# A diffusion step's first stages: finer pieces, column tiles in S5, and its weights made between the short convolutions

## The chip, the cores and the metric

One core of one Trainium2 chip. The metric is the device time of one execution of the whole step, in microseconds (us), median of three runs.

## The reference, cut to what matters

One inference step of a two-layer trunk. Layer 0 (even) mixes 640 tokens (128 of context, 512 latent) with two mixers side by side, a Hyena long convolution and an S5 scan; layer 1 is an mLSTM; each layer has an expert mixer. The change touches what comes before the first expert mixer.

```python
def hyena_filters(n_tok, w1, b1, w2, b2, w3, freq, decay):
    ...
    h = jnp.sin(fr * (z @ _f(w1) + _f(b1)))
    h = jnp.sin(fr * (h @ _f(w2) + _f(b2)))
    h = (h @ _f(w3)) * jnp.exp(-t[:, None] * jnp.abs(_f(decay)))
    h = h.reshape(n_tok, HY_ORDER, 2, HY_WIDTH)
    fwd, bwd = h[:, :, 0], h[:, :, 1]
    kern = jnp.concatenate([fwd, jnp.zeros_like(fwd[:1]), bwd[1:][::-1]], axis=0)
    kern = kern * lax.rsqrt(jnp.sum(kern * kern, axis=0, keepdims=True) + EPS)
    return jnp.fft.rfft(kern, axis=0)

def s5_mix(u, h0_re, h0_im, a_re, a_im, b_re, b_im, c_re, c_im, log_step, d_skip, glu_w, glu_b):
    ...
    lam_bar = jnp.exp(lam * jnp.exp(_f(log_step))[..., None])
    b_bar = ((lam_bar - 1.0) / lam)[..., None] * lax.complex(_f(b_re), _f(b_im))
    ...
    y_f, hf = s5_scan(u, lam_bar[0], b_bar[0], c_mat[0], h0[:, 0])
    y_b, hb = s5_scan(u[:, ::-1], lam_bar[1], b_bar[1], c_mat[1], h0[:, 1])
    y = (y_f + y_b[:, ::-1]).reshape(bsz, n_tok, S5_WIDTH) + _f(d_skip) * u_flat
    y = jax.nn.gelu(y)
    y = y * jax.nn.sigmoid(y @ _f(glu_w) + _f(glu_b))
```

`lam_bar` depends on weights alone: 32 groups of 16 channels with 64 complex states in each of two directions. Beside this, `silu(cond) @ ada_w` gives the scales and shifts of all norms.

## The kernel before, in words

The program is a chain of stages; a stage is a block in which each engine has its own list of instructions, written out by hand, with semaphores between the lists. Nothing reorders a list. The residual stays in the tile `X` (128 x 5 x 1024, f32), the tokens in five tiles of 128.

`start` (L915 to L1232) makes the Hyena filters' spectra, the first quarter of the conditioning and the first norm. PE: two sine layers (L1004), per token tile four raw tap products of 512 columns (L1035) into four banks, with one block of the conditioning (L1015) behind each of the first four; then the context's spectrum (L1058), eight blocks of the DFT (L1072) with the column sums of squares (L1048) between them, and a product that spreads the norms over the partitions (L1080). DVE: the sines' reduction (L1149, L1238 to L1244), the taps (L1158 to L1164), squares (L1171), spectra (L1182), the first norm (L1189, L1192), and last ten multiplications of the spectra `KC`, `KS` by their norms (L1231). ACT: sines, envelopes, copies, square sums of `X` (L1127). POOL adds the position embedding to `X` in one operation (L999).

`even_inputs` (L1262 to L1425) transposes the normed rows into `HT` (L1334), multiplies by 16 blocks of 128 columns of the input weights (L1314, each block 16 matmuls of 320 tokens), convolves the first 12 blocks with three taps on DVE (`short_conv`, L1252 and L1256), turns them on PE (L1325) and places them. The last four blocks are S5's channels; ACT drains each in 16 pieces of 32 x 160 (L1389) that sort the tokens by their place in a chunk of four. After the convolutions DVE makes S5's parameters (`s5_parameters`). `hyena_convolve` follows.

`s5` (L1697 to L2167) works in four quads of groups. For a quad m DVE makes the input weights (`inputs`, L2048 to L2054) and the readout weights (`readouts`, L2071 to L2085), PE transposes the input weights (`turn`), maps chunks into states (`into_states`, L1971), DVE turns the states by angles (`turn_in`, L2095 to L2114), scans them (L2124) and turns back (`scans`, L2136 to L2159, which ends with `prev_set`), PE makes the matrix inside a chunk (`inside`, L1982) and the outputs (`outputs`, L1999, L2002), ACT applies Gelu in 16 pieces (L1892). POOL makes the angles and decays of each quad. Between these steps PE takes the remaining 16 blocks ("rows") of the conditioning product (`ada_row`, L1935), whose weights SP streams from DRAM through two buffers.

DVE's order in `s5` is: inputs(0), diagonal, inputs(1), readouts(0), turn_in(0), scans(0), then for each m turn_in(m), readouts(m), inputs(m + 1), scans(m). PE's is: turn(m), row, into_states(m), row, outputs(m - 1), row, inside(m), row.

`s5_gate` and `project_and_norm` follow; the latter adds the projected mix to `X`.

## Time and profile before

| | |
|---|---|
| median of three runs | 4515.22 us (4513.23 to 4517.06) |
| profiled execution | 4515.3 us, span 4513.5 us |
| mean granted clock of TensorE | 0.968 |
| busy share of the span: PE, DVE, POOL, ACT | 93%, 65%, 36%, 17% |
| `start` | 0 to 150.5 us |
| `even_inputs` | 150.5 to 308.3 us |
| `hyena_convolve` | 308.3 to 412.7 us |
| `s5` | 412.7 to 645.4 us |
| `s5_gate` | 645.4 to 667 us |

### The profile page before, as it was taken

The numbers are of one execution on the slowest core, as the hardware profiler recorded it, in microseconds if no ns is written. First come the engines' busy times: TensorE is split into PE (matmuls) and PEld (weight loads), VectorE is DVE, ScalarE is ACT, GpSimd is POOL, SyncE is SP. The second block draws the span as 40 slices with busy tenths as digits, with TensorE's granted clock in tenths as the row PEclk, the third lists the DMA queues.
The fourth block names the chain that finished last, engine by engine and source line by source line (L and its number), as shares of the span: only waits on it lengthen the run. The fifth ranks groups of instructions, "written<-read, shape, count | busy, mean of one in ns | idle before, by whom it ended". The sixth has DMA issues, their size and how long they took to land. (4 is left out here: it accounts for less than half of the span.)

```text
span 4513.5 us, 44328 instructions
## 1 busy us (share of the span) xinstructions
PE 4206.5 (93%) x15630; PEld 2476.9 (55%) x15630; DVE 2955.5 (65%) x5889; ACT 751.1 (17%) x1583; POOL 1619.6 (36%) x1472
## 2 busy tenths in 40 slices
PE   7785669999999999999989997999999999999998
PEld 3552445768554555545536875576855455554553
DVE  5447953999876766557634227499987676664763
ACT  2121441037000000000002222102810000000000
POOL 1003300028566655545400000001956564554640
PEclk9897889999999999999999999999999999999999
DMA  4111641137999999979921204112789999997993
GB/s 166 52 58 39 228 182 58 56 107 223 364 357 365 410 360 365 353 293 410 350 86 56 70 28 91 41 57 85 223 338 363 366 410 360 363 361 287 406 359 119
DMA packets 354408, 1045.42 MB, mean 232 GB/s; under 512 B 31657, under 2 KB 132361, under 8 KB 343002
## 3 DMA queue, kind: packets, MB, share of 16 engines
q0 software_dynamic: 148096, 545.34, 31.7%
q1 hardware_dynamic: 107036, 447.12, 26.8%
q10 hardware_dynamic: 99072, 50.33, 4.0%
q8 instruction: 116, 1.90, 0.2%
q14 instruction: 88, 0.72, 0.0%
HBM read 988.54 MB, written 54.14 MB: 231 GB/s over the span
## 5 line engine op out<-in xcount | busy, mean ns | idle before, releaser
L592 PE MATMUL banks<-blocks,picked_T 128*128 128x512 f32 x3072 | 1359.1, 594 | 16.0 <-DVE picked_T L772 16.0
L555 PE MATMUL banks<-h_dense_T,blocks 128*128 128x384 f32 x4096 | 1357.6, 486 | 0.0
L555 PEld LDWEIGHTS banks<-h_dense_T,blocks 128*128 128x128 f32 x4096 | 776.9, 190 | 581.9 <-issue 98.5
L592 PEld LDWEIGHTS banks<-blocks,picked_T 128*128 128x128 f32 x3072 | 585.9, 191 | 711.6 <-issue 657.5
L383 POOL DMA_INDIRECT expert_rows<-in_pk_u_dram,expert x512 | 667.3, 1303 | 478.6 <-DVE own_dots L787 253.7
L383 POOL DMA_INDIRECT expert_rows<-in_pk_v_dram,expert x512 | 601.1, 1174 | 514.5 <-DVE acc L806 262.4
L806 DVE SCALAR_TENSOR_TENSOR acc<-expert_rows,expert_weight,acc 128x1024 f32<-128x1024 f32 x504 | 622.8, 1282 | 67.4 <-DMA expert_rows<-in_pk_v_dram,expert 66.8
L787 DVE CUSTOM_DVE_ANT_0 expert_rows<-expert_rows,h_rows 128x1024 f32<-128x1024 f32 x512 | 601.5, 1221 | 59.1 <-DMA expert_rows<-in_pk_u_dram,expert 57.6
L772 DVE TENSOR_TENSOR picked_T<-dense_act,shared 128x384 f32<-128x384 f32 x246 | 209.9, 854 | 569.6 <-PE banks L592 560.1
L408 ACT ACTIVATE dense_act<-banks 128x384 f32<-128x384 f32 x246 | 120.6, 490 | 2229.8 <-PE banks L555 2229.6
L374 POOL TENSOR_SCALAR expert_rows<-iota,picked_T 128x128 f32<-128x128 f32 x384 | 251.2, 672 | 472.7 <-ACT picked_T L414 415.9
L761 DVE TENSOR_SCALAR expert_rows<-iota,picked_T 128x128 f32<-128x128 f32 x768 | 222.0, 364 | 9.7 <-PE banks L581 9.4
L535 PE MATMUL banks<-h_dense_T,blocks 128*128 128x384 f32 x512 | 210.9, 494 | 2.9 <-PEq L107 2.9
L581 PE MATMUL banks<-expert_rows 128*128 128x128 f32 x1536 | 181.8, 277 | 20.0 <-ACT expert_rows L428 11.8
L581 PEld LDWEIGHTS banks<-expert_rows 128*128 128x128 f32 x1536 | 175.8, 192 | 28.8 <-ACT expert_rows L428 16.0
L537 PE MATMUL banks<-shared,blocks 128*128 128x256 f32 x512 | 154.2, 383 | 0.0
L2696 POOL MEMSET VX<- 128x40 f32 x1 | 0.2, 169 | 420.3 <-POOLq L107 420.3
L361 POOL IOTA iota<- 128x16 f32 x2 | 0.3, 146 | 409.8 <-POOLq L107 409.8
L1314 PE MATMUL banks<-HT,MIXT 128*128 128x320 f32 x512 | 140.1, 433 | 1.0 <-ACT HT L1371 1.0
L2464 PE MATMUL banks<-w_block,shared 128*128 128x256 f32 x640 | 138.3, 379 | 0.0
L2443 PE MATMUL banks<-shared,w_block 128*128 128x320 f32 x512 | 138.0, 432 | 0.0
L537 PEld LDWEIGHTS banks<-shared,blocks 128*128 128x128 f32 x512 | 98.6, 193 | 69.6 <-issue 3.3
(495 smaller groups left out, 3788.7 us busy)
## 6 DMA issues: line engine op xcount, KB each, us to landing
blocks<-in_pk_u_turned_dram SPq DMA_DIRECT2D x256, 512.0 KB, 6.6
blocks<-in_pk_v_dram SPq DMA_DIRECT2D x256, 512.0 KB, 6.7
gates_dram<-shared ACTq DMA_DIRECT2D x48, 1024.0 KB, 5.1
shared<-gates_dram SPq DMA_DIRECT2D x32, 1536.0 KB, 11.4
ada_block<-in_ada_rest_dram SPq DMA_DIRECT2D x32, 1280.0 KB, 7.5
blocks<-in_pk_w_q_dram SPq DMA_DIRECT2D x32, 512.0 KB, 3.4
MIXT<-in_ev_w_in_dram SPq DMA_DIRECT2D x16, 512.0 KB
expert_rows<-in_pk_u_dram,expert POOLq DMA_INDIRECT x512, 8.4
```

What stands on the lines that cost most here:

```text
L374: pool.tensor_scalar(hot(first_hot, n), iota128[:], cols[:, z, 0, t:t + 1], None, ALU.is_equal).then_inc(hot_first, 1)
L383: pool.indirect_dma_start(out=rows[:, r % RING, :], out_offset=None, in_=table, in_offset=bass.IndirectOffsetOnAxis(ap=idx[:, x, n % SLOTS ...
L535: pe.matmul(ps[:, at_:at_ + DENSE], lhs, HT[:, k, :], start=(k == 0), stop=(k == KD - 1))
L537: mm = pe.matmul(ps[:, at_ + HALF:at_ + HALF + NR * P], lhs, HTR[:, k, :], start=(k == 0), stop=(k == KD - 1))
L555: mm = pe.matmul(dense_dots(c), u[:, k * P:(k + 1) * P], HT[:, k, :], start=(k == 0), stop=(k == KD - 1))
L581: pe.matmul(ps[:, at_:at_ + P], hot(second_hot, n), hot(first_hot, n), start=True, stop=True).then_inc(spread, 1)
L592: mm = pe.matmul(ps[:, at_:at_ + HALF], wt[:, c % WEIGHED, z * P:(z + 1) * P], v[:, half_ * HALF:(half_ + 1) * HALF], start=(c == 0), stop ...
L761: dve.tensor_scalar(hot(second_hot, n), iota128[:], cols[:, z, 1, t:t + 1], cols[:, z, 2, t:t + 1], ALU.is_equal, ALU.mult).then_inc(hot_s ...
L772: dve.tensor_tensor(wt[:, c % WEIGHED, :], activation_of(c), gate_of[g % 2][:, :, c % KEYS_A_GROUP], ALU.mult).then_inc(weighed, 1)
L787: dve.tensor_tensor_reduce(rows[:, r % RING, :], rows[:, r % RING, :], H[:, x, :], 1.0, 0.0, ALU.mult, ALU.add, dots[:, x, n:n + 1]).then_ ...
L806: ins = dve.scalar_tensor_tensor(out=a, in0=rows[:, r % RING, :], scalar=by, in1=a, op0=ALU.mult, op1=ALU.add)
L1314: mm = pe.matmul(ps[:, at + c * HALF:at + c * HALF + EVEN], lhs, HT[:, k, c * EVEN:(c + 1) * EVEN], start=(k == 0), stop=(k == KD - 1))
```

## The change

1. `start`. The first sine layer waits for three loads on two queues (SP and ACT) instead of six on one; the layers run in halves of 320 columns. Raw taps come in ten units of 2 x 512 columns that rotate through three pairs of banks; envelopes likewise. The position embedding is added by DVE in four pieces between the taps. The last two conditioning blocks follow all raw taps. Squares move from DVE to ACT; the column sums use four column tiles of 32; DVE's steps for the norm are reordered. The ten multiplications of `KC` and `KS` move to the beginning of `even_inputs` on DVE.
2. `even_inputs`. SP first stores `X` to DRAM. DVE's loop over the blocks is written out, and between the twelve convolutions DVE makes S5's parameters, the input weights of all quads (kept in a tile of their own) and the readout weights (kept in `X`'s place). The last four blocks are made by `chunk_products`: 128 matmuls of 32 x 160 in four column tiles, whose moving operand reads every fourth token; ACT drains each block in one operation.
3. `hyena_convolve` reuses a tile in place of one of its own.
4. `s5`. DVE clears `BL`, makes the first quad's angles and the diagonal, and no inputs or readouts; ACT copies these into place (`place_inputs`, `place_readouts`, `begin`). POOL makes the angles of the other quads. The first quad's `into_states` is ahead of its two conditioning rows. Conditioning rows, `inside` and `outputs` use column tiles of 32; their drains are one or two ACT operations instead of 4 or 16, and a row is stored by two transfers.
5. SP loads `X` back from DRAM when the last readouts are placed; DVE waits for that at the beginning of `project_and_norm`.

The core of the diff:

```diff
@@ start
+            act.dma_start(w1[:], T["hy_w1"]).then_inc(first_in, 16)
+            act.dma_start(col[:], T["hy_cols"]).then_inc(first_in, 16)
-            pool.wait_ge(x_in, 32)
-            pool.tensor_tensor(X[:, 1:NT, :], X[:, 1:NT, :], pos, ALU.add).then_inc(x_ready, 1)
+            def raw(u):
+                t, o = divmod(u, 2)
+                if u >= 3:
+                    pe.wait_ge(taps_done, u - 2)
+                for d in range(2):
+                    j, at = 2 * o + d, raw_at(u) + d * HALF
+                    mm = pe.matmul(ps[:, at:at + HALF], h[:, t * P:(t + 1) * P],
+                                   w3[:, j * HYW:(j + 1) * HYW], start=True, stop=True)
+                mm.then_inc(taps_raw, 1)
...
+                    mm = pe.matmul(ps[32 * q:32 * q + 32, SUMS:SUMS + P],
+                                   one_at[:, 31 - row:63 - row], sq[:, n * P:(n + 1) * P],
+                                   start=(t == 0 and n < 4), stop=(t == NT - 1 and n >= 2 * KD - 4))
...
+            for t in range(NT):
+                taps(t)
+                if t == 1:
+                    dve.wait_ge(x_in, 32)
+                if t:
+                    dve.tensor_tensor(X[:, t, :], X[:, t, :], pos[:, t - 1, :], ALU.add
+                                      ).then_inc(x_ready, 1)
@@ even_inputs
+            sp.dma_start(x_dram, X[:]).then_inc(x_kept, 16)
+            def chunk_products(i, b):
+
+                pe.wait_ge(w_in[b], 16 * i + 16)
+                pe.wait_ge(x_out, 2 * i + (b - 1))
+                for n in range(4):
+                    at = (2 * b + n // 2) * HALF + n % 2 * CHUNKS
+                    for k in range(KD):
+                        lhs = w[:, b, k * P + 32 * n:k * P + 32 * n + 32]
+                        for j in range(T4):
+                            mm = pe.matmul(ps[32 * j:32 * j + 32, at:at + CHUNKS], lhs,
+                                           HT[:, k, j::T4], start=(k == 0), stop=(k == KD - 1))
+                mm.then_inc(used, 1)
...
-                for k in range(4):
-                    for j in range(T4):
-                        ins = act.activation(
-                            UP[32 * j:32 * j + 32, m, k, :].rearrange("p (h c) -> p h c", h=2),
-                            src[32 * k:32 * k + 32, :, j::T4], ACT.Copy)
-                ins.then_inc(x_out, 1)
+                act.activation(UP[:, m].rearrange("p (h k) c -> p h (k c)", h=2), src, ACT.Copy
+                               ).then_inc(x_out, 1)
...
+            turns()
+            for c in range(hyena):
+                b = c % 2
+                dve.wait_ge(x_out, c + 1)
+                dve.wait_ge(turned, c + 1)
+                short_conv(dve, line, y[:, b, :], x[:, b, :], lambda k: taps[:, c, k:k + 1])
+                dve.sem_inc(conv_done, 1)
+                dve.sem_inc(x_used, 1)
+                if c == 0:
+                    decays()
+                elif c == 1:
+                    powers()
+                elif c == 2:
+                    weights()
+                elif c < 7:
+                    inputs(c - 3)
+                elif c < 11:
+                    if c == 7:
+                        dve.wait_ge(x_kept, 16)
+                    readouts(c - 7)
@@ s5
+            sp.wait_ge(c_set, 8 * QUADS)
+            sp.dma_start(X[:], x_dram).then_inc(x_in, 16)
+                for j in range(T4):
+                    at = y_at(j)
+                    for i in range(4):
+                        pe.matmul(ps[32 * i:32 * i + 32, at:at + CHUNKS], M[:, i, 32 * j:32 * j + 32],
+                                  UP[:, m, i, :], start=True, stop=False)
+                    for d in range(2):
+                        for part in range(2):
+                            for i in range(4):
+                                mm = pe.matmul(ps[32 * i:32 * i + 32, at:at + CHUNKS],
+                                               CL[:, part, 4 * d + i, 4 - 4 * d + j, :],
+                                               PREV[:, part, 4 * d + i, :], start=False,
+                                               stop=(d == 1 and part == 1))
+                    mm.then_inc(y_raw, 1)
...
+                to = G[:, m, :].rearrange("p (c j) -> p j c", j=T4)
+                for n in range(2):
+                    src = ps[:, y_at(2 * n):y_at(2 * n) + 2 * CHUNKS]
+                    act.activation(to[:, 2 * n:2 * n + 2, :], src.rearrange("p (j c) -> p j c", j=2),
+                                   ACT.Gelu_apprx_tanh).then_inc(y_out, 1)
-            inputs(0)
-            dve.wait_ge(diag_set, 1)
-            inputs(1)
             for m in range(QUADS):
-                if m == 0:
-                    readouts(0)
                 turn_in(m)
-                if m:
-                    readouts(m)
-                    if m + 1 < QUADS:
-                        inputs(m + 1)
                 scans(m)
@@ project_and_norm
+            dve.wait_ge(x_in, 16)
```

PE's list at the end of `even_inputs`, before; `HT` holds the transposed rows, `MIXT` the weights' buffers, `conv_block` a convolved block:

```order
L1314 MATMUL banks<-HT_0,MIXT_0 128x320 x16
L1325 MATMUL banks<-ident_0,conv_block_0 128x128 x5
L1314 MATMUL banks<-HT_0,MIXT_0 128x320 x16
L1325 MATMUL banks<-ident_0,conv_block_0 128x128 x5
L1314 MATMUL banks<-HT_0,MIXT_0 128x320 x32
```

and with the change:

```order
L1392 MATMUL banks<-HT_0,MIXT_0 32x160 x128
L1402 MATMUL banks<-ident_0,conv_block_0 128x128 x5
L1392 MATMUL banks<-HT_0,MIXT_0 32x160 x128
L1402 MATMUL banks<-ident_0,conv_block_0 128x128 x5
L1392 MATMUL banks<-HT_0,MIXT_0 32x160 x256
```

A block of 16 matmuls has become 128, in the same place among the turns.

DVE's list at the beginning of `s5`, before, from the inputs of quad 1 to the first turn (`norm_rows` holds readouts and tables, `s5_w` are work tiles):

```order
L2048 TENSOR_TENSOR s5_w_1_0<-s5_B_0,s5_powers_in_0 128x512
L2049 TENSOR_TENSOR s5_w_3_0<-s5_B_0,s5_powers_in_0 128x512
L2054 TENSOR_TENSOR s5_Bl_0<-s5_w_1_0,s5_w_3_0 64x32x16 x2
L2071 TENSOR_TENSOR s5_w_1_0<-s5_C_0,s5_powers_out_0 128x640
L2072 TENSOR_TENSOR s5_w_3_0<-s5_C_0,s5_powers_out_0 128x640
L2085 TENSOR_TENSOR norm_rows_0<-s5_w_1_0,s5_w_3_0 64x4x5x16 x4
L2078 TENSOR_TENSOR s5_w_1_0<-s5_C_0,s5_powers_out_0 128x640
L2079 TENSOR_TENSOR s5_w_3_0<-s5_negC_0,s5_powers_out_0 128x640
L2085 TENSOR_TENSOR norm_rows_0<-s5_w_3_0,s5_w_1_0 64x4x5x16 x4
L2095 TENSOR_TENSOR s5_w_0_0<-MIXT_0,norm_rows_0 128x8x32
```

and with the change, from the second operation of the stage to the first of the turn (the angles are L2217 to L2224):

```order
L2217 TENSOR_TENSOR norm_rows_1<-s5_steps_0,s5_turns_0 128x1024
L2218 TENSOR_SCALAR norm_rows_1<-norm_rows_1 128x1024
L2219 TENSOR_SCALAR norm_rows_1<-norm_rows_1 128x1024
L2220 TENSOR_TENSOR norm_rows_1<-s5_steps_0,s5_turns_0 128x1024
L2221 TENSOR_TENSOR norm_rows_1<-s5_steps_0,s5_turns_0 128x1024
L2222 TENSOR_TENSOR norm_rows_1<-norm_rows_1 128x1024
L2223 TENSOR_TENSOR norm_rows_1<-norm_rows_1 128x1024
L2224 TENSOR_SCALAR norm_rows_1<-norm_rows_1 128x1024
L2227 MEMSET states_before_0 128x2x4
L2228 MEMSET states_before_0 128x2x4
L2229 TENSOR_TENSOR s5_diag_0<-ident_0,s5_d_0 32x512
L2239 TENSOR_TENSOR s5_w_0_0<-MIXT_0,norm_rows_1 128x8x32
```

The inputs and readouts have left this list; the angles have come to it from POOL's.

DVE's list in `even_inputs` with the change, from one convolution past a quad's readouts to the next (before, there was nothing between two convolutions but a copy of the taps):

```order
L1306 TENSOR_SCALAR conv_block_0<-conv_source_0,conv_taps_0 128x640
L1310 SCALAR_TENSOR_TENSOR conv_block_0<-conv_source_0,conv_taps_0,conv_block_0 128x127
L1310 SCALAR_TENSOR_TENSOR conv_block_0<-conv_source_0,conv_taps_0,conv_block_0 128x511
L1310 SCALAR_TENSOR_TENSOR conv_block_0<-conv_source_0,conv_taps_0,conv_block_0 128x127
L1310 SCALAR_TENSOR_TENSOR conv_block_0<-conv_source_0,conv_taps_0,conv_block_0 128x511
L1586 TENSOR_TENSOR MIXT_0<-s5_C_0,s5_powers_out_0 128x640
L1587 TENSOR_TENSOR MIXT_0<-s5_C_0,s5_powers_out_0 128x640
L1588 TENSOR_TENSOR X_0<-MIXT_0 128x640
L1589 TENSOR_TENSOR MIXT_0<-s5_C_0,s5_powers_out_0 128x640
L1590 TENSOR_TENSOR MIXT_0<-s5_C_0,s5_powers_out_0 128x640
L1591 SCALAR_TENSOR_TENSOR X_0<-MIXT_0 128x640
L1306 TENSOR_SCALAR conv_block_0<-conv_source_0,conv_taps_0 128x640
```

Six operations of readouts, two of which write `X`, have come in between.

## Rows read from the trace of the kernel before

**Rows 1.** The page's chain that ended last: share of the span by line.

```profile
PE banks L555 15%; PE banks L592 15%; ACT expert_rows L423 1%; PE banks L581 0%; DVE top_index L646 0%; DVE top_index L650 0%; PE banks L535 0%; DVE rest L647 0%; DMA gates_dram<-shared 0%; ACT shared L441 0%; DVE top_value L644 0%; DVE top_value L649 0%; PE banks L537 0%; ACT expert_rows L428 0%; DVE best_at L646 0%
```

**Rows 2.** Windows by stage: length, busy PE, PEld, DVE, ACT, POOL; clock, DMA, GB/s.

```profile
0.00:150.50 150.50, 99.29 (x576) 49.29 (x576) 92.95 (x88) 34.84 (x52) 13.61 (x13) 0.87 0.33 124
150.50:308.30 157.80, 151.07 (x612) 109.41 (x612) 55.09 (x182) 42.79 (x114) 0.00 (x0) 0.99 0.25 79
...
412.70:645.40 232.70, 130.64 (x1666) 92.49 (x1666) 196.22 (x242) 108.09 (x276) 83.69 (x43) 0.76 0.50 187
```

**Rows 3.** Timeline of `start`, the sine layers: PE, DVE, ACT.

```profile
8.34 1.96 PE L1004 MATMUL banks<-features,hy_w 33*64 33x512 f32 x2 [8.34 <-DMA hy_times<-in_hy_times_dram]
...
10.86 0.94 DVE L1149 TENSOR_SCALAR sine_arg<-banks,hy_cols 64x640 f32<-64x640 f32 x1 [2.29 <-PE banks L1005]
...
22.71 0.74 ACT L1093 ACTIVATE sine<-sine_arg 64x640 f32<-64x640 f32 x1 [6.77 <-DVEq L1152]
```

**Rows 4.** Timeline of `start`, the taps: DVE and POOL.

```profile
30.79 1.22 DVE L1158 TENSOR_TENSOR taps<-banks,envelope 128x1024 f32<-128x1024 f32 x1 [8.17 <-PE banks L1035]
...
41.18 9.47 POOL L999 TENSOR_TENSOR X<-X,MIXT 128x4096 f32<-128x4096 f32 x1
...
41.87 9.87 DVE L1164 TENSOR_TENSOR taps<-taps,bwd_taps 128x1024 f32<-128x1024 f32 x1
...
72.69 1.22 DVE L1164 TENSOR_TENSOR taps<-taps,bwd_taps 128x1024 f32<-128x1024 f32 x1
```

**Rows 5.** Timeline of `start`, sums, DFT, spread and the last multiplications.

```profile
84.14 3.67 PE L1048 MATMUL banks<-envelope,one_column 128*16 128x128 f32 x32
...
87.74 3.70 PE L1072 MATMUL banks<-taps,cos_fwd 128*128 128x512 f32 x8
...
127.45 3.69 PE L1080 MATMUL banks<-envelope,ones 16*128 16x512 f32 x8
...
137.93 1.22 DVE L1231 TENSOR_TENSOR KC<-KC,banks 128x1024 f32<-128x1024 f32 x1
```

**Rows 6.** Timeline of `even_inputs`: PE and SP at its start, DVE, ACT's last drain.

```profile
150.59 5.92 PE L1334 MATMUL banks<-ident,MIXT 128*128 128x128 f32 x40 [19.44 <-PEq L107]
157.51 14.80 PE L1314 MATMUL banks<-HT,MIXT 128*128 128x320 f32 x54 [1.00 <-ACT HT L1371]
...
153.92 0.81 SPq L1291 DMA_DIRECT2D MIXT<-in_ev_w_in_dram  x2
...
184.46 0.61 DVE L1252 TENSOR_SCALAR conv_block<-conv_source,conv_taps_cur 128x640 f32<-128x640 f32 x1 [5.07 <-ACT conv_source L1356]
...
302.70 4.88 ACT L1389 ACTIVATE US<-banks 32x160 f32<-32x160 f32 x16 [3.72 <-PE banks L1314]
```

**Rows 7.** The page's DMA issues: count, size, time to landing.

```profile
gates_dram<-shared ACTq DMA_DIRECT2D x48, 1024.0 KB, 5.1
...
ada_block<-in_ada_rest_dram SPq DMA_DIRECT2D x32, 1280.0 KB, 7.5
```

**Rows 8.** Timeline of `s5`: DVE, and ACT's last Gelu.

```profile
419.75 0.69 DVE L2048 TENSOR_TENSOR s_w<-s_B,s_powers_in 128x512 f32<-128x512 f32 x1 [6.87 <-POOL norm_rows L1795]
...
461.86 5.97 DVE L2095 TENSOR_TENSOR s_w<-MIXT,norm_rows 128x256 f32<-128x256 f32 x8 [0.25 <-DVE norm_rows L2085]
...
476.82 8.90 DVE L2095 TENSOR_TENSOR s_w<-s_w,norm_rows 128x256 f32<-128x256 f32 x6
...
616.34 4.62 DVE L2095 TENSOR_TENSOR s_w<-s_w,norm_rows 128x256 f32<-128x256 f32 x6
...
626.18 0.16 DVE L2159 TENSOR_TENSOR s_states<-s_w 128x8 f32<-128x8 f32 x1
...
634.55 7.42 ACT L1892 ACTIVATE US<-banks 32x160 f32<-32x160 f32 x16 [14.41 <-PE banks L2002]
```

**Rows 9.** Timeline of `s5`: PE's matmuls in column tiles.

```profile
466.94 1.93 PE L1982 MATMUL banks<-norm_rows,s_Bl 128*32 128x224 f32 x32
...
593.66 1.27 PE L1935 MATMUL banks<-ada_block,cond_s 128*2 128x160 f32 x32
```

More of the change, by code:

```diff
@@ L1153, in _ @@
[L1153 to L1163 removed]
+            line.then(dve.memset(one_at[:, 31:32], 1.0))
@@ new lines, in _ @@
+            dve.wait_ge(first_in, 3 * 16)
+            for n in range(4):
+                layer, half = divmod(n, 2)
+                dve.wait_ge(layer_done, n + 1)
+                if layer:
+                    dve.wait_ge(sines_done, half + 1)
+                line.then(dve.tensor_scalar(arg[:, half], ps[0:HYF, n * HALF:n * HALF + EVEN],
+                                            col[:, layer:layer + 1], col[:, 2:3], ALU.add, ALU.mult))
+                reduce_turns(dve, line, arg[:, half], turn[:, half])
+                dve.sem_inc(args_ready, 1)
@@ L1250, in short_conv @@
+    line.then(dve.tensor_scalar(arg, arg, PI_BELOW, -PI_BELOW, ALU.min, ALU.max))
 def short_conv(dve, line, out, x, taps):
@@ L1408, in _ @@
             line = Line(dve, dve_line)
+            for t in range(NT):
+                at = (4 + 2 * group_of(t)) * HALF
+                for K in (KC, KS):
+                    v = K[:, t].rearrange("p o c -> p (o c)")
+                    line.count(dve.tensor_tensor(v, v, ps[:, at:at + 2 * HALF], ALU.mult))
+            line.settle()
             dve.wait_ge(rows_turned, 2 * NT)
@@ new lines, in inputs @@
+            def inputs(m):
+                size, k = [P, 8, T4, S5C], slice(8 * m, 8 * m + 8)
+                t1, t2 = (t[:, 0:8 * T4 * S5C].rearrange("p (k s j) -> p k s j", k=8, j=S5C)
+                          for t in (part1, part2))
+                p_re, p_im = (pb[:, part, k, :].unsqueeze(3).to_broadcast(size) for part in range(2))
+                b_re, b_im = (B[:, part, k, :].unsqueeze(2).to_broadcast(size) for part in range(2))
+                for part, (f1, f2, op) in enumerate(((p_re, p_im, ALU.subtract),
+                                                     (p_im, p_re, ALU.add))):
+                    line.count(tt(t1, b_re, f1, ALU.mult))
+                    one(tt(t2, b_im, f2, ALU.mult))
+                    one(tt(s.inputs[:, part, k], t1, t2, op))
@@ new lines, in readouts @@
+            def readouts(m):
+                size, k = [P, 8, T4 + 1, S5C], slice(8 * m, 8 * m + 8)
+                t1, t2 = (t.rearrange("p (k s j) -> p k s j", k=8, j=S5C) for t in (part1, part2))
+                p_re, p_im = (pc[:, part, k, :].unsqueeze(3).to_broadcast(size) for part in range(2))
+                c_re, c_im = (C[:, part, k, :].unsqueeze(2).to_broadcast(size) for part in range(2))
+                line.count(tt(t1, c_re, p_re, ALU.mult))
+                one(tt(t2, c_im, p_im, ALU.mult))
+                one(tt(outs[:, 0, k], t1, t2, ALU.subtract))
+                line.count(tt(t1, c_re, p_im, ALU.mult))
+                one(tt(t2, c_im, p_re, ALU.mult))
+                one(dve.scalar_tensor_tensor(out=outs[:, 1, k], in0=t1, scalar=-1.0, in1=t2,
+                                             op0=ALU.mult, op1=ALU.subtract))
@@ L1747, in half_of, with factors @@
             return slice(64 * gr, 64 * gr + 64)
+        wide = [P, 8, LAT_CHUNKS]
+        def factors(m):
+            return (hl[:, c, quad(m)].unsqueeze(2).to_broadcast(wide) for c in range(3))
         def cols_of(gr):
@@ L1826, in decays @@
                     ins.then_inc(a_set, 1)
-            for m in range(QUADS):
+            decays(0)
+            for m in range(1, QUADS):
                 angles(m)
@@ new lines, in first_angles @@
+            def first_angles():
+                s = steps[:, :].unsqueeze(1).to_broadcast(wide)
+                both, hi, lo = factors(0)
+                one(tt(turns[:], s, both, ALU.mult))
+                one(ts(turns[:], turns[:], 1.0, ROUND, ALU.mult, ALU.add))
+                one(ts(turns[:], turns[:], 1.0, -ROUND, ALU.mult, ALU.add))
+                line.count(tt(ang[:], s, hi, ALU.mult))
+                one(tt(low[:], s, lo, ALU.mult))
+                one(tt(ang[:], ang[:], turns[:], ALU.subtract))
+                one(tt(ang[:], ang[:], low[:], ALU.add))
+                ts(ang[:], ang[:], 0.5, -0.5, ALU.min, ALU.max).then_inc(angle_set, 1)
```

766 lines of the change are left out of this document (377 added, 389 removed).

## The prediction

> **What bounds the kernel now.** I read the windows by stage first, then each touched stage in order of time, and the page's last chain to see what is not touched. All times are in the profiled run, 4515.3 us, whose span is 4513.5 us, so 1.8 us lie outside; the median of the three runs is 4515.22 us, so the profiled execution may stand for it. The chain that ended last is mostly the experts' matmuls, L555 and L592 [rows 1]; they come after 667 us and the change leaves them alone. What can move is the first 645 us. There the windows show three kinds of bound [rows 2]. In `start` (150.5 us) PE and DVE are busy 99 and 93 us, neither full: they wait for each other. In `even_inputs` (157.8 us) PE is busy 151 us, so only PE's own work or its start and end count. In `s5` (232.7 us) DVE is busy 196 us and PE 131 us at a mean clock of 0.76: DVE leads, with PE's slow clock close behind.
>
> **The change, stage by stage.**
>
> `start`, head. The first sine matmul waited until 8.34 us for the last of six loads; each layer is then PE, six DVE operations on 640 columns, and ACT, one after the other, and the second layer's sine ends at 23.45 [rows 3]. Now three small loads on two queues are enough, and halves of 320 columns overlap PE, DVE and ACT. I take 3.5 us from the load and 4 us from the overlap (each layer is 7.5 us now; of its 4.05 us on DVE little shrinks). Sines done near 16 us: **-7.5**.
>
> `start`, taps. Five tiles take from 23.5 to 73.9 us, the end of the last DVE operation (72.69 + 1.22) [rows 4], 50 us, though DVE works 4 operations of 1.22 to 1.27, 4.95 us, a tile. PE may only refill its four banks when DVE has emptied them, and one DVE operation took 9.87 us while POOL's 9.47 us addition ran [rows 4]. Now units of 512 columns rotate through three pairs of banks, and POOL's addition becomes four DVE pieces of about 1.22. DVE's sum is 5 x (2 x (0.69 + 0.70) + 2.44) + 4 x 1.22 = 31 us, where 0.69 is DVE's time for 512 columns estimated as half of 1.22 with its fixed part. Ten pairs of raw matmuls at 0.92 (a quarter of the 3.70 of eight records, [rows 5]) and two modulations stay under that. The first taps start 3 us after the sines instead of 7, as one raw pair is enough. From 19 us, 31 of DVE and some waits: about 53 us instead of 73.9, **-21 in all, -13.5 of it here**.
>
> `start`, spectra. From 73.9 to 137.9 us eight DFT blocks of 3.70, five column sums of 3.67 with gaps of about 1, the 3.69 spread and DVE's norms pass [rows 5]. Each sum becomes the same 32 records in four column tiles, one quarter of the time if they overlap: 5 x 2.6 = **-13**. The rest is the order: the squares go to ACT, and the normalisations are moved forward, so that they no longer follow the last DFT: PE's sum is 5 for the context, 8 x 3.7, 5 x 2 for sums with gaps, 3.7, 48 us, and DVE's (spectra 10.6, norms 12.5, the rest 7) is 31. So the stage ends near 53 + 48 + 1 = 102 us, if DVE does not hold PE. Last, ten multiplications, 11.4 us from 137.93 to the end [rows 5], move to the next stage. 150.5 - 102 = **-48** in all; bounds: -38 (PE at half its clock for a third of it, or DVE late) to -53.
>
> `even_inputs`, added. The ten multiplications run on DVE while PE transposes (5.92 us) and makes the first products (54 records in 14.80, so 8.8 for a block of 32) [rows 6]: DVE had nothing before its first convolution [rows 6], and the 26 small operations that follow may delay that convolution by a few us, of which PE's two-block lead takes 9: 0. The weights, inputs and readouts are six DVE operations of 0.7 to 0.83 between two convolutions, 4.1 to 5 us, against 5.07 us of idle time there [rows 6]: 0. If that cover is short, PE's turn of the block, a block later, is what is late. SP stores the 2560 KB residual ahead of the weights' loads, which now land 3.6 us after their issue [rows 6]. At the rate of the `ada` stream (1280 KB twice in 7.5 us) the store and the two 512 KB loads need 10.5 us, at that of the `gates` store (1024 KB in 5.1 us) 17.8 [rows 7], against 6.9 from stage start to first product: +3.6 to +11, taken **+4**, since SP's queue reads at the first rate.
>
> `even_inputs`, the last four blocks. Each block is 32 records of 320 columns in 8.8 us; now 256 records of 160 columns, four at a time. The nearest row of that form is the `ada` product, 32 records of 160 columns in four column tiles in 1.27 us, 0.040 each [rows 9]: 10.2 us, +1.4 a block, **+5.6**. The rows of 32-wide weights, 1.93 us for 32 of 224 columns, 0.060 each [rows 9], would make it 15.4, +26 in all; I keep that as the high end, and 0 as the low one. The drain of the last block, 4.88 us of ACT after the last product [rows 6], becomes one operation of 0.7: **-4.2**.
>
> The Trainium skill speaks a little against this: its page "TensorE: Matmul & The Clock Gate" ("Why this matters for your kernels") measured 2.38 times, not 3, for three column tiles of 32 columns, which as an estimate makes 8.8 x 3 / 2.38 = 11.1 us a block and the forecast 4424 instead of 4421; the rows' 0.040 and 0.060 a record have that value between them.
>
> `s5`, head. DVE waits 6.87 us for POOL's clearing, makes two quads' inputs, the diagonal and the readouts, and begins its first turn at 461.86 us, 49.1 us into the stage [rows 8]. All of that is gone from DVE but the diagonal; added are a clearing (about 4.3 us) and the eight angle operations (about 8). The path is now clearing, two ACT copies of about 1.1, PE's turn 2, four copies, PE's states 6, with ACT's three table operations, about 1.1 each by its 0.74 for 640 columns [rows 3], and a table load before the last: about 22 us. **-27**.
>
> `s5`, quads. From the first turn to the last `prev_set` DVE needs 461.86 to 626.34, 164.5 us, 41 a quad [rows 8]. Without readouts and inputs and the eight little copies, a quad of DVE is turn and scans, 15 (461.86 to 476.82), and the rest, 10 without POOL (616.34 to 626.34) and up to about twice that beside it (8.90 us for the six products that take 4.62 alone) [rows 8]: 25 to 35. PE's quad is 130.6 / 4 = 33 us at its clock now [rows 2], and gains the tiles: outputs 160 records x 0.040 = 6.4, inside 160 of about 0.032 = 5.1 instead of 1.93 [rows 9]; some 37 us. Four `ada` rows need two loads each: 7.5 us to landing and 1.3 of use [rows 7, 9], 35 us. So PE and the stream take over from DVE, at about 40 us a quad with their waits. Three such periods and one quad of DVE (25): 145. **-19.5**.
>
> `s5`, tail. From 626.34 to 645.4, 19 us: the last Gelu, 7.42 us in 16 pieces [rows 8], becomes two operations of about 0.8. **-6**. `s5`: -52.5; bounds: -25 (half clock, 46 a quad and a slower tail) to -66 (35 a quad).
>
> The residual's reload, 2560 KB, is issued after the last readouts and lands long before `project_and_norm` asks for it, but it stands before `w_out`: 0 to +4, taken **+1**.
>
> Sum: -48 + 4 + 5.6 - 4.2 - 52.5 + 1 = -94. 4515.3 - 94 = **4421 us**.
>
> **The rivals.**
> (a) *The strided moving operand.* The last four blocks read every fourth token, one f32 in 16 bytes. ACT writes such steps in the Gelu row: 160 columns in 0.46 us [rows 8], long for its size, but no PE row here reads with a step. If PE's rate is halved by it, a block costs 8.8 more: +35, **4456**. The Trainium skill, "SBUF — State Buffer" ("Door 1: The DMA port swizzle"), says that two accesses must hit a 16-byte line for full rate, and these hit each line once; no row here shows it for PE. Against it speaks that a block's 32 records of 320 columns take 8.8 us, 0.86 ns a column, two cycles at 2.4 GHz, which leaves a step some room.
> (b) *`s5` stays as long between its quads.* PE was at a clock of 0.76 with gaps; more, shorter matmuls and no DVE slack could leave it at the lower level. At 49 us a quad it is 4 x 9 us more than I have, -16.5 instead of -52.5: **4457**.
> (c) *The column tiles run one after the other.* Then a record of 160 columns costs 0.137 us (160 of these 0.86 ns): a block 35 us, 25 more than I have; in each quad of `s5` outputs and inside need 22 and 15 us instead of 6.4 and 5.1, +25 on the engine that leads there; the sums of `start` gain nothing, +13. 4421 + 4 x 25 + 4 x 25 + 13 = **4634**, slower. Over 4 x 256 + 4 x 320 records, the gain of 94 us is used up once each takes about 0.04 us more than I have, from 0.08 on. Both rows of column tiles are below that, 0.040 and 0.060 [rows 9].
> (d) *`start` keeps its length*: the pieces wait for the same loads and for each other, and half clock doubles the raws. Only the 11.4 us of multiplications leave it: 48 - 11.4 less, **4458**.
>
> **How the numbers follow.** My case 0.72, (a) 0.09, (b) 0.09, (c) 0.03, (d) 0.04, others 0.03. The forecast is 4421. My own bounds together are -26 to -120; all of them at once on one side is unlikely, but (a), (b) and (d) end at 4456 to 4458, so the range is 4392 to 4462. A change of 0.2%, 9 us, is what a measurement of this kernel can tell from none. Slower is (c) and half of the others: 0.04; same 0.02; faster 0.94.
>
> **What would show it.** In the profile after: first sine matmul near 5 us; the last taps near 53; `even_inputs` starting near 102, with first products some 11 us after it; 256-record groups of about 10 us (19 would be (a), 35 (c)) and one ACT operation behind the last; the first DVE turn of `s5` about 22 us into its stage; quads of about 40 us in which DVE waits for PE; the stage near 180 us. Wrong would be DVE still full in `s5`, POOL's angles stretching it as now; a first product 20 us into `even_inputs`; or a wait of `project_and_norm` for the residual.

## The result and the profile after

The changed kernel takes **4473.57 us** (median of 4 runs, 4471.03 to 4474.17) against 4516.14 us (4513.23 to 4517.91) for the kernel before, run beside it: a ratio of 0.9905, 95% interval 0.9888 to 0.9922. It is faster, by 43 us where 94 were forecast, and lies outside the range on the slow side. Its profiled execution took 4474.17 us, with a span of 4472.4 us and a mean granted clock of 0.972.

The stages, each from its first instruction on PE or DVE to that of the next, in the two profiled executions:

| stage | before, us | after, us | difference | forecast |
|---|---|---|---|---|
| `start` | 150.5 | 104.9 | -45.6 | -48 |
| `even_inputs` | 157.8 | 201.8 | +44.0 | +5.4 |
| `hyena_convolve` | 104.4 | 101.7 | -2.7 | 0 |
| `s5` | 232.7 | 189.9 | -42.8 | -52.5 |
| gate and project (to the first L535) | 103.9 | 107.0 | +3.1 | +1 |
| the rest | 3764.2 | 3767.1 | +2.9 | 0 |

The same windows as [rows 2], of the changed kernel (`start`, `even_inputs`, `hyena_convolve`, `s5`):

```profile
0.00:104.90 104.90, 84.57 (x576) 37.60 (x576) 69.48 (x95) 46.31 (x69) 4.14 (x12) 0.93 0.45 178
104.90:306.68 201.78, 193.73 (x1509) 132.25 (x1509) 99.23 (x227) 27.00 (x54) 0.00 (x0) 0.97 0.21 76
306.68:408.35 101.67, 73.94 (x164) 31.92 (x164) 74.30 (x70) 7.12 (x9) 0.92 (x1) 0.87 0.00 0
408.35:598.29 189.94, 143.60 (x2627) 113.04 (x2627) 118.98 (x141) 77.58 (x168) 55.37 (x34) 0.79 0.66 243
```

In `even_inputs` PE is busy 193.7 us instead of 151.1 at a clock of 0.97: most of the stage's 44 us are longer work, not longer waits. In `s5` DVE fell from 196 to 119 us, so it no longer leads. The timeline shows where PE's 43 us are. After the last convolved block come S5's four blocks, and behind them ACT's drain of the last:

```profile
224.71 4.47 PE L1378 MATMUL banks<-HT,MIXT 128*128 128x320 f32 x16
...
229.70 18.50 PE L1392 MATMUL banks<-HT,MIXT 128*32 128x160 f32 x256
...
248.86 18.59 PE L1392 MATMUL banks<-HT,MIXT 128*32 128x160 f32 x256
...
268.11 36.99 PE L1392 MATMUL banks<-HT,MIXT 128*32 128x160 f32 x512
...
305.18 0.70 ACT L1470 ACTIVATE US<-banks 128x640 f32<-128x640 f32 x1 [17.76 <-PE banks L1392]
```

A block of 256 records takes 18.5 us, 0.0723 us a record, where 32 records of the old form take about 8.8 ([rows 6]: 54 in 14.80). Four times 9.7 is 39 us. A window from 229.70 to 248.00 us shows PE busy for all of its 18.3 us at a granted clock of 1.00, so neither a wait nor the clock is in it. The drain fell from 4.88 to 0.70 as forecast.

The start of the stage (PE and SP) answers to the first rows of [rows 6]:

```profile
104.93 0.32 SPq L1351 DMA_DIRECT2D residual_dram<-X  x1
...
107.81 1.64 SPq L1355 DMA_DIRECT2D MIXT<-in_ev_w_in_dram  x2
...
117.60 7.73 PE L1378 MATMUL banks<-HT,MIXT 128*128 128x320 f32 x18 [6.40 <-DMA MIXT<-in_ev_w_in_dram]
```

PE has its weights 9.8 us after their issue instead of within 3.6; the first product comes 12.7 us into the stage instead of 7.0 [rows 6], +5.7. Nor is that all: behind the wait of 6.4 us the granted clock fell, as the window from 117.60 shows (0.65, 19 records in 7.7 us):

```profile
117.60:125.30 7.70, 7.70 (x19) 5.17 (x20) 2.92 (x17) 0.00 (x0) 0.00 (x0) 0.65 0.32 125
```

The 96 records of the first three blocks take 28.72 us, against 26.11 before, where the clock stood at 1.00 in the window from 157.51: +2.6. Wait, clock, blocks and drain make 5.7 + 2.6 + 39 - 4.2 = 43 of the stage's 44 us.

In `start` the ends of the taps and the context's two spectra (DVE, ACT, PE):

```profile
53.13 1.22 DVE L1224 TENSOR_TENSOR taps<-taps,bwd_taps 128x1024 f32<-128x1024 f32 x1
53.14 1.98 PE L1084 MATMUL banks<-taps,cos_fwd 128*128 128x512 f32 x4
54.49 1.23 DVE L1232 TENSOR_TENSOR X<-X,MIXT 128x1024 f32<-128x1024 f32 x1
55.81 1.06 ACT L1170 ACTIVATE MIXT<-X 128x1024 f32<-128x1024 f32 x1 [4.86 <-DVE X L1232]
...
56.99 2.32 ACT L1119 ACTIVATE mod_rows<-banks 2x128 f32<-2x128 f32 x8
...
59.33 1.08 ACT L1178 ACTIVATE KC<-banks 128x512 f32<-128x512 f32 x2
59.98 3.78 PE L1084 MATMUL banks<-taps,sin_fwd 128*128 128x512 f32 x4 [4.86 <-ACT KC L1178]
...
67.77 1.08 PE L1048 MATMUL banks<-envelope,one_column 128*32 128x128 f32 x32
```

The last taps end at 54.4 us instead of 73.9 [rows 4], and a column sum takes 1.08 us instead of 3.67 [rows 5]. But a new wait stands there: ACT stood 4.86 us for DVE's last addition to `X`, took its square and the conditioning's copies, and only then the copies of the context's spectrum, for which PE stood 4.86 us. Behind that wait, too, the clock was the lower one: the second product (L1084) took 3.78 us, where the first, of the same shape, took 1.98.

```profile
59.98:63.76 3.78, 3.78 (x5) 1.66 (x6) 0.00 (x0) 1.04 (x2) 0.00 (x0) 0.50 0.68 222
```

In `s5` the four beginnings of a DVE turn (line, tile as in [rows 8]):

```profile
431.39 11.98 DVE L2239 TENSOR_TENSOR s_w<-MIXT,norm_rows 128x256 f32<-128x256 f32 x8 [9.93 <-ACT MIXT L1998]
...
483.67 5.97 DVE L2239 TENSOR_TENSOR s_w<-MIXT,norm_rows 128x256 f32<-128x256 f32 x8 [20.59 <-ACT MIXT L1998]
...
525.85 5.97 DVE L2239 TENSOR_TENSOR s_w<-MIXT,norm_rows 128x256 f32<-128x256 f32 x8 [16.13 <-ACT MIXT L1998]
...
561.48 5.97 DVE L2239 TENSOR_TENSOR s_w<-MIXT,norm_rows 128x256 f32<-128x256 f32 x8 [9.93 <-ACT MIXT L1998]
```

The first turn stands 23 us into the stage (49.1 before). The periods are 52.3, 42.2 and 35.6 us, and DVE waits 10 to 21 us before each turn for ACT, which waits for PE. PE in turn waits for the conditioning's stream; the waits of the stage (total us, times, longest):

```profile
DVE s_w L2239 <- ACT MIXT L1998: 56.6, 4, 20.6
...
PE banks L2101 <- DMA ada_block<-in_ada_rest_dram: 16.0, 8, 3.4
```

The stream itself stands still at the head of the stage. SP issues its first two loads at 407.4 and 408.1 us; the third, which needs a buffer that PE has used, comes 24 us later (this row is the second and the third):

```profile
408.14 24.29 SPq L1885 DMA_DIRECT2D ada_block<-in_ada_rest_dram  x2
```

### The profile page after: what moved, and what is told of

Read it like the earlier page. It is cut to its first block and busy times, and to the rows that moved or that the text cites. A ratio compares the mean times of both kernels' runs of the same rounds, so it can differ in the third digit from the quotient of the medians.

```text
span 4472.4 us, 47773 instructions
## 1 busy us (share of the span) xinstructions
PE 4248.3 (95%) x17486; PEld 2509.9 (56%) x17486; DVE 2899.0 (65%) x5840; ACT 716.7 (16%) x1432; POOL 1592.1 (36%) x1462
## 5 line engine op out<-in xcount | busy, mean ns | idle before, releaser
L535 PE MATMUL banks<-h_dense_T,blocks 128*128 128x384 f32 x512 | 210.7, 494 | 2.9 <-PEq L107 2.9
```

The costliest lines, as they stand in the source:

```text
L535: pe.matmul(ps[:, at_:at_ + DENSE], lhs, HT[:, k, :], start=(k == 0), stop=(k == KD - 1))
```

## The experiments

Two questions: why a block takes 18.5 us, and what the `X` store, the stream in `s5` and the order at the end of `start` cost. The kernel before, run beside each of the three batches, took 4517.60, 4516.23 and 4517.38 us, so that medians of different batches can be compared within some 1.4 us.

**Batch 1: the blocks.** *e1_together* leaves the column tiles and takes the step out of the moving operand, which then reads 160 tokens that lie together (so S5's channels get the wrong tokens):

```diff
-                                           HT[:, k, j::T4], start=(k == 0), stop=(k == KD - 1))
+                                           HT[:, k, j * CHUNKS:(j + 1) * CHUNKS],
+                                           start=(k == 0), stop=(k == KD - 1))
```

> The moving operand of the last four blocks is 160 neighbouring columns instead of every fourth token (the tokens of S5's chunks are then the wrong ones); same counts, same weights, same tiles. Theory S, the step of the moving operand: a block of 256 records goes from 18.5 to about 10.2 us (0.040 a record, as the ada rows), the whole kernel from 4474 to about 4441 us. Rival W, the loading of 32-wide weights, 256 times a block, sets the pace: the block stays at 18.5 us and the kernel at 4474. Rival T, four column tiles at a time simply overlap only by half in this stage: also 18.5 us.

Measured: 4432.51 us (4430.18 to 4435.8), ratio to before 0.9812 (0.9796 to 0.9829). The block:

```profile
230.46 8.90 PE L1392 MATMUL banks<-HT,MIXT 128*32 128x160 f32 x256
```

*e2_strides* gives the first three blocks steps of 1, 2 and 3, and makes the last without column tiles but with the step of 4: 128 x 128 weights, 160 columns, 64 records (the first three blocks read the wrong tokens).

```diff
+                step = 1 + 2 * (i - hyena // 2) + b
...
-                                           HT[:, k, j::T4], start=(k == 0), stop=(k == KD - 1))
+                                           HT[:, k, j:j + step * CHUNKS:step],
+                                           start=(k == 0), stop=(k == KD - 1))
```

> The four last blocks take four different moving operands: block 1 step 1, block 2 step 2, block 3 step 3 (all in column tiles, 256 records), block 4 step 4 with 128-wide weights and no column tiles (64 records of 160 columns). S5's inputs are then the wrong tokens. Theory S, if the cost comes with crossing to a new 16-byte line at each column: block 1 10.2 us, block 2 10.2 (two columns a line), block 3 between 10 and 18.5, block 4 17.6 instead of 8.8. If any step costs the same, blocks 2 and 3 are 18.5 each. Rival C, the four tiles read against each other and a step alone costs nothing: block 4 takes 8.8 us. Rival W: blocks 1 to 3 all 18.5.

Measured: 4452.56 us in a single run. The four blocks:

```profile
235.42 8.93 PE L1403 MATMUL banks<-HT,MIXT 128*32 128x160 f32 x256
...
245.02 9.63 PE L1403 MATMUL banks<-HT,MIXT 128*32 128x160 f32 x256
...
255.31 14.13 PE L1403 MATMUL banks<-HT,MIXT 128*32 128x160 f32 x256
...
269.38 18.38 PE L1390 MATMUL banks<-HT,MIXT 128*128 128x160 f32 x64
```

The step costs: 8.93, 9.63 and 14.13 us for steps of 1, 2 and 3 in the same 256 records, and 18.38 us for a step of 4 with no column tile at all, so the tiles are not needed for the loss. Contiguous column tiles cost almost nothing: 8.9 us against 8.78 for the whole-width form.

*e3_products_back* undoes the blocks alone (the old products and the drain in 16 pieces):

```diff
-                chunk_products(hyena // 2, b)
+                products(hyena // 2, b)
```

> The last four blocks are made as before the change (16 matmuls of 128 by 320) and drained in 16 pieces; all else as changed. Block 8.78 us instead of 18.5, the last drain 4.9 us instead of 0.7: 4474 - 39 + 4 = 4439 us under every theory that puts the loss into these blocks. If the loss were in the work that DVE got between the convolutions, the stage would stay near 200 us and the kernel near 4474.

Measured: 4435.68 us (4431.6 to 4446.15), ratio 0.9826 (0.9809 to 0.9842), 38 us less than the changed kernel: that is what the new form of these blocks and of their drain costs. The second block, the last two together, and the last drain (PE, ACT):

```profile
238.48 8.78 PE L1378 MATMUL banks<-HT,MIXT 128*128 128x320 f32 x32
...
247.68 17.39 PE L1378 MATMUL banks<-HT,MIXT 128*128 128x320 f32 x64
...
265.11 4.88 ACT L1472 ACTIVATE US<-banks 32x160 f32<-32x160 f32 x16 [3.73 <-PE banks L1378]
```

*e4_by_place* keeps the column tiles and pays the step elsewhere. ACT writes `HT` in the order of the tokens' place in their chunk, so that PE reads contiguous columns for all blocks, and ACT's drains of the convolved blocks put the tokens back with a stepped write:

```diff
-                act.activation(HT[:, 4 * q:4 * q + 4, t * P:(t + 1) * P],
-                               ps[:, at:at + HALF].rearrange("p (k c) -> p k c", k=4),
+                to = HT[:, 4 * q:4 * q + 4, :].rearrange("p k (j c) -> p k j c", j=T4)
+                act.activation(to[:, :, :, t * (P // T4):(t + 1) * (P // T4)],
+                               ps[:, at:at + HALF].rearrange("p (k c j) -> p k j c", k=4, j=T4),
...
-                    ins = act.activation(OUT[:, n, c * EVEN:(c + 1) * EVEN], ps[:, at:at + EVEN],
+                    to = OUT[:, n, :].rearrange("p (c j) -> p j c", j=T4)[:, 2 * c:2 * c + 2, :]
+                    ins = act.activation(to, ps[:, at:at + EVEN].rearrange("p (j c) -> p j c", j=2),
```

> The transposed rows are written in the order of a chunk's place (all first tokens, then all second, and so on), so that the moving operand of the column tiles is contiguous; the Hyena blocks' drains put the tokens back in order. Theory S: a block at 10.2 us, ACT's copies up to twice as long but beside PE: 4441 to 4444 us. Rivals W and T: 18.5 us a block, 4474.

Measured: 4432.75 us (4430.61 to 4436.94), ratio 0.9816 (0.98 to 0.9832); blocks of 8.90 us. The stepped drains take 0.77 us instead of 0.44 each, on an engine that waits there. The batches below build on this kernel.

**Batch 2: store, stream, additions.** *f1_store_later* moves the store of `X` on SP's queue from ahead of the stage's first loads to behind them.

```diff
-            sp.dma_start(x_dram, X[:]).then_inc(x_kept, 16)
...
                 sp.dma_start(dst[:], T[src]).then_inc(par_in, 16)
+            sp.dma_start(x_dram, X[:]).then_inc(x_kept, 16)
```

> On top of the version with the rows ordered by place (4432.75 us): SP stores the residual behind the first loads of the stage instead of ahead of them. If the store delays the first products, as I put it (they start 12.8 us after the stage, PE waiting 6.55 us for its weights), PE's first product comes some 5 us earlier and the kernel goes to about 4427 us. Rival: the loads' latency at the start of the stage is what PE waits for whatever is ahead of them, or DVE's chain of multiplications and parameters takes the place of the wait: 4432 to 4433 us.

Measured: 4423.32 us (4419.82 to 4438.75), ratio 0.9804 (0.9784 to 0.9825). PE's first product, with its wait:

```profile
112.09 13.19 PE L1378 MATMUL banks<-HT,MIXT 128*128 128x320 f32 x48 [0.86 <-ACT HT L1450]
```

It comes 5.8 us earlier than in e4_by_place (117.93) and no longer waits for the weights, and the clock behind it is the full one:

```profile
112.09:119.80 7.71, 7.71 (x29) 5.50 (x30) 6.40 (x16) 0.00 (x0) 0.00 (x0) 1.00 1.02 366
```

The 96 records of the first three blocks take 26.11 us, as in the kernel before. The store ahead of the loads was the cause of both, 5.8 and 2.6 us; the medians differ by 9.4.

*f2_half_bytes* loads half of each conditioning block in `s5`, and PE uses that half twice (the conditioning rows made here lack the other half of their weights).

```diff
-                sp.dma_start(ada[:, n % 2, :], w[:, n % 2, :]).then_inc(ada_in[n % 2], 16)
+                sp.dma_start(ada[:, n % 2, 0:KD // 4 * MOD_W], w[:, n % 2, 0:KD // 4 * MOD_W]
+                             ).then_inc(ada_in[n % 2], 16)
...
-                            at = k * MOD_W + ADA_COLS * j
+                            at = k % 2 * MOD_W + ADA_COLS * j
```

> On top of the same version: each of the 32 loads of conditioning weights in S5 brings half of its bytes, and PE uses that half twice (the conditioning rows made there are then wrong); the instructions of PE, ACT and DVE stay the same. Theory M, the stream and its two buffers stretch the quads beyond the 40 us that I forecast: PE's 24 us of waiting for these loads go, the s5 stage goes from 190 to about 168 us, the kernel from 4433 to about 4410. Rival K, PE's half clock and its chain with ACT and DVE set the quads: the waits only move elsewhere, at most 5 us go.

Measured: 4417.73 us (4416.98 to 4420.65), ratio 0.9785 (0.9769 to 0.9802), 15 us under e4_by_place. In the traces `s5` goes from 186.3 to 176.0 us. PE's waits for the stream in e4_by_place:

```profile
PE banks L2103 <- DMA ada_block<-in_ada_rest_dram: 14.9, 9, 3.2
PE banks L2103 <- DMA ada_bias<-in_ada_b_dram: 8.9, 3, 4.2
```

and with half the bytes:

```profile
PE banks L2104 <- DMA ada_block<-in_ada_rest_dram: 2.9, 3, 1.2
PE banks L2104 <- DMA ada_bias<-in_ada_b_dram: 2.6, 1, 2.6
```

DVE's second turn, in the same run:

```profile
437.03 3.63 DVE L2242 TENSOR_TENSOR s_w<-MIXT,norm_rows 128x256 f32<-128x256 f32 x4 [0.35 <-DVE s_states L2299]
```

It follows DVE's own last operation by 0.35 us (19.06 us of waiting in e4_by_place). PE's waits for the stream fell from 23.8 to 5.5 us, by 18, and the time by 10 (this stage in the traces) to 15 (the medians): the stream holds the stage by that much, less than theory M said and more than rival K, and where it doesn't, DVE leads.

*f3_pool_adds* gives the additions to `X` back to POOL, in one operation as before.

```diff
+            pool.tensor_tensor(X[:, 1:NT, :], X[:, 1:NT, :], pos, ALU.add).then_inc(x_ready, NT - 1)
...
-                    dve.tensor_tensor(X[:, t, :], X[:, t, :], pos[:, t - 1, :], ALU.add
```

> On top of the same version: the position embedding is added by POOL in one operation, as before the change, and DVE's four pieces of 1.22 us are gone. Theory P, as I priced it: DVE's taps, which read two tiles in SBUF, stand still while POOL's addition of about 9.5 us runs; they lose about 8.5 us and save 4.9, so the stage is about 4 us longer, 4436 to 4437 us. Rival: DVE's 9.87 us operation in the kernel before had another cause, and the stage is up to 5 us shorter, 4428 us.

Measured: 4429.52 us (4421.12 to 4431.23), ratio 0.9811 (0.9794 to 0.9827). POOL's operation and DVE's beside it:

```profile
35.99 8.84 POOL L1006 TENSOR_TENSOR X<-X,MIXT 128x4096 f32<-128x4096 f32 x1
...
38.57 7.36 DVE L1225 TENSOR_TENSOR taps<-taps,bwd_taps 128x1024 f32<-128x1024 f32 x1
45.85 1.21 DVE L1226 TENSOR_TENSOR taps<-taps,bwd_taps 128x1024 f32<-128x1024 f32 x1
```

The collision is back (7.36 us for an operation of 1.21; it ends 1.1 us after POOL's), and DVE's last tap is later, 58.4 us instead of 54.4. Yet the stage ended at 103.0 us, 2.2 earlier than in e4_by_place: ACT no longer found the last addition to `X` in its way, PE did not stand for the context's copies, and its second context product took 1.98 us instead of 3.78. This run was a miss of mine, and it pointed at ACT's order, which batch 3 tests.

**Batch 3: two orders.** *g1_copies_first* is f1_store_later with the last square of `X` moved on ACT behind the copies of the context's spectrum.

```diff
-            for t in range(NT):
+            for t in range(NT - 1):
+                x_square(t)
             mod_copy(2)
             mod_copy(3)
...
                                ).then_inc(ctx_out, 1)
+            x_square(NT - 1)
             squares(0)
```

> f1_store_later with one piece of the start's ScalarE list moved: the square of X's last token tile comes behind the four context copies instead of ahead of them (its place ahead made the context copies wait for VectorE's last X add; TensorE stood 4.86 us for the second context product in the changed kernel's trace). Order theory: TensorE's wait for KC in the start falls from 4.9 us to under 1, the stage ends 3 to 5 us earlier, and the kernel takes about 4419 us (4417 to 4421) where f1_store_later took 4423.3. Rival, VectorE sets the stage's end: its last taps and the X add before them stay where they are, the wait shows up again behind the odd products, and the time stays at 4423 (4421.5 to 4425).

Measured: 4415.47 us (4412.89 to 4419.72), ratio 0.9777 (0.9761 to 0.9794). PE, and ACT's copy between, at the place of the wait:

```profile
53.14 1.98 PE L1084 MATMUL banks<-taps,cos_fwd 128*128 128x512 f32 x4
...
54.45 1.31 ACT L1181 ACTIVATE KC<-banks 128x512 f32<-128x512 f32 x2
...
55.10 1.99 PE L1084 MATMUL banks<-taps,sin_fwd 128*128 128x512 f32 x4
...
60.74 1.08 PE L1048 MATMUL banks<-envelope,one_column 128*32 128x128 f32 x32
...
97.95 6.23 PE L1415 MATMUL banks<-ident,MIXT 128*128 128x128 f32 x40 [3.63 <-PEq L107]
```

The wait is gone, and with it the low clock behind it. The second product's windows in f1_store_later and here:

```profile
59.94:63.72 3.78, 3.78 (x5) 1.67 (x6) 0.00 (x0) 1.03 (x2) 0.00 (x0) 0.50 0.80 252
...
55.10:57.10 2.00, 2.00 (x6) 0.80 (x6) 0.63 (x1) 1.19 (x2) 0.00 (x0) 1.00 0.61 227
```

The first sum comes 7.1 us earlier than in f1_store_later, and the stage ends at 97.95 instead of 105.00 us, more than the 3 to 5 us that I had taken from the one wait: 4.8 are the wait, and the other 2.2 are the products behind it, which ran at the lower clock. The order theory holds; VectorE does not set the end.

*g2_row_first* is g1_copies_first with one conditioning row of quad 0 moved from behind `into_states(0)` to ahead of it, as in the other quads (on PE; on ACT its copy likewise).

```diff
-                if m == 0:
-                    into_states(m)
-                    n = ada_rows(n, 2)
-                else:
-                    n = ada_rows(n, 1)
-                    into_states(m)
-                    n = ada_rows(n, 1)
+                n = ada_rows(n, 1)
+                into_states(m)
+                n = ada_rows(n, 1)
```

> g1_copies_first with quad 0 of the S5 stage in the order of the other quads: one conditioning row between turn(0) and into_states(0) instead of two behind it, on TensorE and ScalarE. Stream theory (the conditioning blocks' two buffers hold the stage back; e4_by_place stood 14.9 + 8.9 us for them): the stream starts moving some 8 us earlier, every later wait for a block shrinks by as much until VectorE leads, and the stage is 4 to 8 us shorter than in g1_copies_first. Rival, the head of the stage leads: a row's two halves (2.36 us each at half clock) stand ahead of into_states(0) and make everything behind it 2 to 5 us later, the stream only waits elsewhere; 0 to 5 us longer than g1_copies_first.

Measured: **4408.25 us** (4405.91 to 4412.31), ratio 0.976 (0.9744 to 0.9777), 7 us under g1_copies_first and 65 under the changed kernel. DVE's first two turns:

```profile
378.80 12.79 DVE L2238 TENSOR_TENSOR s_w<-MIXT,norm_rows 128x256 f32<-128x256 f32 x8 [9.26 <-ACT MIXT L2004]
...
423.25 5.97 DVE L2238 TENSOR_TENSOR s_w<-MIXT,norm_rows 128x256 f32<-128x256 f32 x8 [0.35 <-DVE s_states L2295]
```

The first is where it was (378.72), the second follows DVE's own work, PE's waits for the stream fall from 20.4 to 14.3 us, and `s5` takes 177.5 us instead of 182.4. The rival, a later head, fell. How much the order is worth is less sure. The two kernels' times do not overlap (4412.31 us at most here, 4412.89 at least there), but in the two traces, which differ by 5.8 us, only 2.5 us lie before the experts (their first product is at 641.0 instead of 643.5 us), since the gate and projection take 2.7 longer; the other 3.3 lie in the experts, whose code is the same. And `s5` with the same lists took 182 to 190 us over the profiled executions of the runs above (not f2, not g2), so single stages are known to some us only.

## Why the prediction was wrong

**The step that failed is the price of S5's blocks**, "32 records of 160 columns in four column tiles in 1.27 us, 0.040 each [rows 9]: 10.2 us, +1.4 a block, **+5.6**". It measured 18.5 us a block, +9.7, +39. I took the nearest row by the form of the weights (column tiles) and not by the form of the moving operand: the row of [rows 9] reads 160 columns that lie together, the new blocks read one in four. Even the price for contiguous columns was not the fault: in e1_together a record takes 0.035 us. The step makes 33 of the 53 us by which the sum failed, and it is shown from both sides: without the step (e1_together) and without the blocks (e3_products_back) the kernel takes 4433 and 4436 us.

**Rival (a) named this mechanism and its price (+35; the measured difference to the term is 33), and I gave it 0.09.** The argument against it failed: "0.86 ns a column, two cycles at 2.4 GHz, which leaves a step some room". It leaves none at a step of 4: a block took 18.5 us instead of 8.9, a factor of 2.08. The Trainium skill, "SBUF — State Buffer" ("Door 1: The DMA port swizzle"), has the rule that full rate wants two accesses to a 16-byte line. The runs nearly agree: a step of 2, two f32 to a line, costs 8%, a step of 4, one to a line, some 107%, and 3 lies between at 58%. Where no row of the trace has the form that a change brings in, a mechanism with a price and a place deserves more than 0.09 against an argument from clock cycles.

The opposite doubt, rival (c), was idle: four contiguous column tiles take 8.90 us where the whole width takes 8.78, so they overlap 4 x 8.78 / 8.90 = 3.95 times. The prediction's estimate of 11.1 us a block from the 2.38 of "TensorE: Matmul & The Clock Gate" (the Trainium skill, "Why this matters for your kernels") is not borne out: contiguous, a block takes 8.90 us.

**`start`, -48 against -45.6.** The sines (first at 3.80 us, last end at 17.2 us), the taps (54.4 us, forecast 53) and the sums (1.08 us each) came as worked out. I had written "if DVE does not hold PE", but the holder was ACT: by its list, not by its load. g1_copies_first puts it at 7 us, 2.2 of them the low clock behind the wait. One reading in the working was wrong without weight: a pair of raw matmuls is four records, 1.85 us by the 3.70 of eight, not 0.92; ten pairs and two modulations still stay under DVE's 31.

**The store, +4 against +5.7**, within the bounds; the +2.6 of PE's clock behind its wait was no term of mine. f1_store_later takes back both. The multiplications and S5's parameters on DVE cost nothing, as said: the turns of the convolved blocks on PE follow its products without a gap.

**`s5`, -52.5 against -42.8.** The head came as forecast (first turn 23 us into the stage, 22 said). The quads take 43.4 us on the mean instead of 40, because I laid the stream's 35 us beside PE's 37 and added 3 for waits. But the stream has two buffers: after its first two loads it stands until PE has used one, and nothing of it was used in the 23 us of the head. PE then met an unready block 8 times. Half the bytes are worth 10 to 15 us (f2_half_bytes), an earlier first row 2 to 7 (g2_row_first). Rival (b), 49 us a quad, did not come; its price took 4 x 9 us where the forecast counts three such periods, so it was 9 us too high.

No wait for the reloaded residual shows in the gate and projection, so the +1 for it was not needed. Their +3.1 is PE's: the same products keep it busy for 96.7 us instead of 93.5, at granted clocks of 0.87 and 0.95 in the two stages instead of 0.93 and 0.97. No term had that, and what lowered the clock there stays open. The -2.7 in `hyena_convolve` has no term either, but 1.8 of it can be seen: before, PE stood 5.7 us ahead of the stage's first product, which took 3.75 us at a granted clock of 0.50; behind the shorter drain it stands 1.6 us, and the same product takes 1.96 at 1.00. The +2.9 in the experts I didn't try. The experts' part is the same code in all runs, and the traces show it at 3762 to 3768 us: of a difference of 3 us in one execution nothing can be said.

## What to carry to other kernels

Take the price of a matmul from a row whose moving operand has the same step, not only the same shape; where a stage needs every fourth token, let the engine that drains write in that order and PE read contiguously. After a change shortens a stage, read the order of the engines' lists at its new end: here one square ahead of four copies cost 7 us, and one row's place at the head of `s5` another 2 to 7. Price a wait of PE with what its clock does behind it. A store put ahead of loads on one queue costs what it delays the first of them.

## What the hardware showed that I had not expected

The step of an f32 moving operand costs PE little at 2 (9.63 us for 8.93), then 14.13 at 3 and 18.5 at 4, all in column tiles; at 4 it is 18.38 without them. The clock of the blocks of step 4 was 1.00. As an estimate, these times fit a count of the groups of four neighbouring f32 that the 160 columns of a record touch: 160 at a step of 4, 120 at 3 and 80 at 2, and 18.5 us shrunk in that proportion is 13.9 and 9.3. That this is the reason is argued from the four steps and not tested further. ACT's stepped drains cost less than that: 0.77 us for 0.44. And a wait of PE cost more than its length: 6.4 us cost 2.6 behind them, at a granted clock of 0.65, and 4.86 us some 2.2, at 0.50; without the waits (f1_store_later, g1_copies_first) the clock was 1.00 in both places.
